# Linear attention of a two-block network: both directions' scores added before they meet the values, two heads' states on halves of the array in turn, and GpSimd as a fourth worker

## The reference, cut to what matters

```python
la_f = jax.nn.log_sigmoid((r_f @ w_decay_up[0] + b_decay[0])) / GATE_NORMALIZER      # and la_b likewise
def gla_scan(q, k, v, log_a, h0, with_output):
    b = jnp.cumsum(chunked(log_a), axis=3)
    kv = jnp.einsum('bhncd,bhnce->bhnde', kc * jnp.exp(b_last - b), vc)
    decay = jnp.exp(b_last[:, :, :, 0, :])
    # scan over chunks: state = dec_n * state + kv_n; `starts` are the states ahead of each chunk
    inter = jnp.einsum('bhncd,bhnde->bhnce', qc * jnp.exp(b), starts)
    scores = jnp.einsum('bhnid,bhnjd->bhnij', qc * jnp.exp(b - mid), kc * jnp.exp(mid - b))
    intra = jnp.einsum('bhnij,bhnje->bhnie', jnp.where(lower, scores, 0.0), vc)
    return inter + intra, final
o = o_f + rev(o_b)
o = rms_norm_2(o, gla_norm_g)        # then o * silu(g), projections, a pooling branch, merge gates, w_out
```

## Time and profile before

| | us |
|---|---|
| three runs | 4045.81, 4053.06, 4835.9; median 4053.06 |
| the profiled execution | 4056.88, its span 4055.1 |
| linear attention stage and head sums, span's 3081.40 to 3242.13 | 160.7 |
| of these, TensorE in the two head blocks | 24.4 and 25.9 |

### The profile page before, as it was taken

How to read it: one execution, slowest core, us unless ns; L and a number is a source line. 1 busy time by engine, 2 the same in 40 slices (tenths; PEclk the granted TensorE clock), 3 DMA queues, 4 the chain that set the end, 5 groups by cost and what they waited for, 6 DMA issues and landing times.

```text
span 4055.1 us, 70686 instructions
## 1 busy us (share of the span) xinstructions
PE 3674.8 (91%) x31176; PEld 2713.0 (67%) x31176; DVE 1650.1 (41%) x3233; ACT 1207.1 (30%) x2395; POOL 335.1 (8%) x512
## 2 busy tenths in 40 slices
PE   6999998999997997999999997999988898898886
PEld 2565567788885696888888886578877676532222
DVE  1253345433334443556665564344344274311112
ACT  2242033312223232444544443233343232100001
POOL 0000122000001002212121121000010001000000
PEclk9999999999998998999999999799999699889998
DMA  5293053211112010000000000222221022599996
GB/s 183 86 345 133 21 187 104 83 63 63 63 63 80 24 40 8 4 4 4 4 4 4 3 4 35 98 98 89 83 65 58 21 96 97 203 353 387 386 387 245
DMA packets 209521, 433.83 MB, mean 107 GB/s; under 512 B 4976, under 2 KB 5584, under 8 KB 208832
## 3 DMA queue, kind: packets, MB, share of 16 engines
q1 hardware_dynamic: 203952, 413.44, 28.3%
q0 software_dynamic: 5264, 15.87, 1.3%
HBM read 424.05 MB, written 5.24 MB: 106 GB/s over the span
## 4 chain that ended last, share of the span: by engine, by line
PE 75%; DVE 9%; DMA 7%; ACT 4%; SPq 3%; issue 1%; POOL 1%; DVEq 0%; ACTq 0%; POOLq 0%
PE ps L760 14%; PE ps L1918 7%; PE ps L1919 7%; PE ps L1920 7%; PE ps L2336 6%; PE ps L707 4%; PE ps L3642 3%; PE ps L690 3%; DMA part<-in_wg 3%; SPq L193 3%; PE ps L2326 2%; DMA part<-in_wd 2%; PE ps L996 1%; DMA part<-in_wu 1%; PE ps L2454 1%
## 5 line engine op out<-in xcount | busy, mean ns | idle before, releaser
L760 PE MATMUL ps<-part 128*128 128x512 f32 (+1 forms) x3312 | 631.5, 354 | 28.1 <-DVE part L981 10.9
L760 PEld LDWEIGHTS ps<-part 128*128 128x128 f32 x3312 | 538.9, 195 | 122.6 <-DVE part L981 12.1
L1918 PE MATMUL ps<-part 128*128 128x512 f32 (+1 forms) x1536 | 549.9, 358 | 18.0 <-DVE part L1965 11.4
L1919 PE MATMUL ps<-part 128*128 128x512 f32 (+1 forms) x1536 | 549.2, 358 | 0.0
L1920 PE MATMUL ps<-part 128*128 128x512 f32 (+1 forms) x1536 | 549.0, 357 | 0.0
L3642 PE MATMUL ps<-part 128*64 128x512 f32 x1536 | 383.2, 618 | 71.5 <-DMA part<-in_wd 29.9
L2336 PE MATMUL ps<-part 64*64 64x64 f32 x10752 | 365.9, 220 | 20.0 <-DVE part L2615 11.6
L2336 PEld LDWEIGHTS ps<-part 64*64 64x64 f32 x10752 | 334.5, 135 | 49.7 <-DVE part L2615 16.6
L1942 DVE TENSOR_TENSOR part<-part 128x1024 fp32r<-128x1024 f32 x128 | 158.4, 1237 | 496.6 <-ACT part L1931 496.6
L1918 PEld LDWEIGHTS ps<-part 128*128 128x128 f32 x1536 | 290.3, 189 | 68.0 <-DVE part L1965 12.6
L3642 PEld LDWEIGHTS ps<-part 128*64 128x64 f32 x1536 | 115.5, 141 | 320.3 <-issue 214.9
(11 more groups left out here) (423 smaller groups left out, 5050.7 us busy)
## 6 DMA issues: line engine op xcount, KB each, us to landing
part<-in_ada_w SPq DMA_DIRECT2D x36, 2048.0 KB, 9.0
part<-in_mlp_w SPq DMA_DIRECT2D x32, 2048.0 KB, 8.2
part<-in_wg SPq DMA_DIRECT2D x32, 2048.0 KB, 19.9
part<-in_wu SPq DMA_DIRECT2D x32, 2048.0 KB, 19.9
part<-in_wd SPq DMA_DIRECT2D x32, 2048.0 KB, 20.0
part<-in_b_in SPq DMA_DIRECT2D x8, 2048.0 KB, 8.3
part<-in_ab_w_in SPq DMA_DIRECT2D x7, 2048.0 KB, 8.8
part<-in_rkv SPq DMA_DIRECT2D x6, 2048.0 KB, 7.9
```

Of the source, the lines that this page charges most:

```text
L760: mm = pe.e.matmul(ps[:, j * n:j * n + n], lhs, rhs, start=k == ks[0] and i == 0, stop=k == ks[-1] and i == 2)
L1918: pe.e.matmul(ps, wh[:, k, :], hi[:, k, x0:x1], start=k == 0, stop=False)
L1919: pe.e.matmul(ps, wh[:, k, :], lo[:, k, x0:x1], start=False, stop=False)
```

## The change

1. **Heads.** The scores of both directions are added by GpSimd ("g scores sum") into `g.SC[0]` and `g.SC[1]`, and TensorE makes one product of values with scores for each head and 128 tokens instead of two. The two heads of a pair are made together: their state products alternate between the upper and the lower half of the array's rows, into two banks.
2. **GpSimd** takes the products of `q1` and `qm` with the queries, the sums above, clearing of two score tiles, and the second parts 6 to 9 of the weights (`Split.pool`).
3. **Logits.** ScalarE takes the absolute value straight from PSUM with the bias added (two instructions), VectorE adds the bias and takes the minimum with zero in one, so the later subtraction is a plain one.
4. **Order on TensorE.** Two gate pieces stand in turn 0, one in each turn between scores and kv, and one ahead of each head block; the transposes follow the decay logits at once. The head sums move: those of heads 0 and 1 behind kv of turn 3, those of heads 2 and 3 behind the first piece of the merge stage.
5. **Order on ScalarE and VectorE.** The masked copy of the scores comes first in a turn on VectorE. ScalarE copies the gates at the end of a turn; it copies heads 0 and 1 out in turn 3, and squares them behind that turn's exponentials; roots are taken for two heads together. VectorE scales all four heads at the stage's end.

```diff
+    def pool(self, g):                       # class Split
+        pool.wait_ge(self.K.at(name, "rounded", g))
+        pool.e.tensor_tensor(self.rest(g), self.tile(g), self.first(g), SUB).then_inc(*pool.up((name, "split", g)))
...
+GATES_IN = (2, 1, 2, 1, 2)
...
+        if step == 0:
             next(gates)
-        if step:
+            next(gates)
+        else:
...
-            pe.wait_ge(K.at("g km", dm))
+            pe.wait_ge(K.at("g qm", dm), K.at("g km", dm))
...
-            if step < 4:
-                next(gates)
+            next(gates)
...
+            if step == 3:
+                for hd in range(2):
+                    head_sum(K, hd)
             if dm % 2:
...
+                next(gates)
+                heads_pe(K, dm, m)
...
+def heads_pe(K, dm, m):
+    pe.wait_ge(K.at("g scores sum", dm))
+    out = [K.bank("g head", 2 * m + hh) for hh in range(2)]
+    pe.wait_ge(K.at("g states", dm), K.at("g q1", dm))
+    for x in range(4):
+        c = slice(x * 128, x * 128 + 128)
+        for hh in range(2):
+            hd = 2 * m + hh
+            pe.e.matmul(out[hh][:, c], g.vR[:, x, hd * 128:hd * 128 + 128], g.SC[hh][:, x, :], start=True, stop=False,
+                        skip_group_check=True)
+        for e in range(2):
+            for n in (2 * x, 2 * x + 1):
+                o64 = slice(n * 64, n * 64 + 64)
+                for hh, o in halves():
+                    mm = pe.e.matmul(out[hh][:, o64], g.ST[e][o, n, :], g.q1[(dm - 1 + e) % 3][o, o64], start=False,
+                                     stop=e == 1, skip_group_check=True)
...
-            s.e.activation(g.e1, g.la, ACT.Abs).then_inc(*s.up())
+            for pi, (a, b) in enumerate(BOTH):
+                s.wait_ge(K.at("g decay", step, pi))
+                s.e.activation(g.e1[:, a:b], K.ps.of("g decay", step, pi)[:, 0:b - a], ACT.Abs, bias=bias).then_inc(
+                    *s.up(("g abs", step, pi), free("g decay", step, pi)))
...
+        if step == 3:
+            head(0)
...
+        if step == 3:
+            head_squares(0)
+        for _ in range(GATES_IN[step]):
             gate()
...
+        if step == 3:
+            head_rstd(0)
+    head(2)
+    head_squares(2)
+    head_rstd(2)
...
+def gla_pool(K):
+    for step in range(5):
+        if step < 4:
+            pool.wait_ge(K.at("g q1 exp", step))
+            pool.e.tensor_tensor(g.q1[step % 3], g.q1[step % 3], g.qT[:, m, :], MUL).then_inc(*pool.up(("g q1", step)))
+        if step in (2, 4):
+            for hh in range(2):
+                pool.wait_ge(K.at("g scores in", dm, hh), K.at("g scores in", dm - 1, hh))
+                pool.e.tensor_tensor(g.SC[hh], g.SC[hh], g.SC[2 + hh], ADD).then_inc(*pool.up(("g scores sum", dm)))
+        if step < 4:
+            pool.wait_ge(K.at("g qm exp", step))
+            pool.e.tensor_tensor(g.qm[step % 2], g.qm[step % 2], g.qT[:, m, :], MUL).then_inc(*pool.up(("g qm", step)))
+        if step == 2:
+            pool.wait_ge(K.at("g head", 0), K.at("g head", 1))
+            for hh in range(2):
+                pool.e.memset(g.SC[hh], 0.0).then_inc(*pool.up(("g scores empty",)))
+        if step != 1:
+            w.pool((6, None, 7, 8, 9)[step])
...
-def merge_pe(K, gates):
+def merge_pe(K):
+    first = w.columns(8, "gp", 0, x, LAT, lambda k: {})
+    next(first)
+    for hd in (2, 3):
+        head_sum(K, hd)
+    through(first)
```

More of the change, by code:

```diff
@@ L3117, in gla_pe @@
[L3117 to L3120 removed]
+                next(gates)
+                heads_pe(K, dm, m)
+def heads_pe(K, dm, m):
+    g, pe = K.g2, K.pe
+    pe.wait_ge(K.at("g scores sum", dm))
[13 more added lines that the diff above has]
+                                     stop=e == 1, skip_group_check=True)
+                    if x == 3 and e == 1 and n == 7:
+                        mm.then_inc(*pe.up(("g head", 2 * m + hh)))
@@ L3123, in gla_act, with head_sum @@
+def head_sum(K, hd):
+    pe = K.pe
+    ps = K.bank("g head sum", hd)
+    pe.wait_ge(K.at("g head sq", hd))
+    pe.e.matmul(ps, K.ones, K.g2.sq1[hd % 2], start=True, stop=True).then_inc(*pe.up(("g head sum", hd)))
 def gla_act(K):
@@ L3127, in gate, with head, head_squares, head_rstd @@
     def gate():
-        m = next(gates, None)
-        if m is not None:
-            s.wait_ge(K.at("gm", m, 0))
-            s.e.activation(g.G1[:, m, :], K.ps.of("gm", m, 0), ACT.Copy).then_inc(*s.up(("gate raw", m), free("gm", m, 0)))
-            if m % 2:
-                w.act(6 + m // 2)
+        m = next(gates)
+        s.wait_ge(K.at("gm", m, 0))
+        s.e.activation(g.G1[:, m, :], K.ps.of("gm", m, 0), ACT.Copy).then_inc(*s.up(("gate raw", m), free("gm", m, 0)))
+        if m % 2:
+            w.act(6 + m // 2)
+    def head(hd0):
+        for hd in (hd0, hd0 + 1):
+            s.wait_ge(K.at("g head", hd))
+            s.e.activation(g.og[:, hd, :], K.ps.of("g head", hd), ACT.Copy).then_inc(
+                *s.up(("g head in", hd), free("g head", hd)))
+    def head_squares(hd0):
+        for hd in (hd0, hd0 + 1):
+            s.wait_ge(K.at("g head in", hd), K.at("g head gated", hd - 2) if hd >= 2 else {})
+            s.e.activation(g.sq1[hd % 2], g.og[:, hd, :], ACT.Square).then_inc(*s.up(("g head sq", hd)))
+    def head_rstd(hd0):
+        s.ln_exp()
+        for hd in (hd0, hd0 + 1):
+            s.wait_ge(K.at("g head sum", hd))
+            s.e.activation(g.sq1[hd % 2], K.ps.of("g head sum", hd), ACT.Ln, scale=1.0 / 128, bias=K.eps[:, 0:1]).then_inc(
+                *s.up(free("g head sum", hd)))
+        s.wait_ge(s.now())
+        for hd in (hd0, hd0 + 1):
+            s.e.activation(g.sq1[hd % 2], g.sq1[hd % 2], ACT.Exp, scale=-0.5).then_inc(*s.up(("g head rstd", hd)))
     for step in range(5):
@@ L3138, in gla_act @@
             d, m = DM[step]
[L3139 removed]
+            bias = g.n2[:, 29 + 2 * d + m:30 + 2 * d + m]
             if step:
@@ L3275, in merge_pool @@
     K.load(K.pool, K.po.pw, K.D["pool_w"].rearrange("g c d -> c g d"), "merge", "pw")
-def merge_pe(K, gates):
+def merge_pe(K):
     g, p, pe, w, x = K.g2, K.po, K.pe, b2(K), b2_h(K)
-    through(gates)
-    for t in range(2):
-        through(w.columns(8 + t, "gp", 2 * t, x, LAT, lambda k: {}))
+    first = w.columns(8, "gp", 0, x, LAT, lambda k: {})
[3 more added lines that the diff above has]
+    through(first)
+    through(w.columns(9, "gp", 2, x, LAT, lambda k: {}))
     for t in range(2):
```

89 lines of the change are left out of this document (24 added, 65 removed).

## The result

| | before | after |
|---|---|---|
| median, us | 4053.82 (four runs) | 4000.59 (3993.59 to 4008.23, four runs) |
| ratio | | 0.9868, 95% interval 0.9839 to 0.9897 |
| profiled execution, its span | 4056.88, 4055.1 | 3993.59, 3991.8 |
| first decay logit to first product with pool_w | 252.04 | 198.32 |

The changed kernel is 53 us faster, 1.3%, clear of no change, but less than the 2% from which a kernel is called faster here; 4003 was forecast. (One of the four runs of the kernel before, 4835.9, is disturbed and is left out of the ratio.)

What follows compares the result with a forecast made beforehand. TensorE, busy 91% of the span, was taken as the bound, through half-clock head blocks and each turn's engine ring. The stage's 277.5 to 227.1 saves 50.4 us: 4056.9 becomes 4006.5, less 3.8 gives 4003; range 3986 to 4028.

Steps and rivals of the forecast that it cites:

- TensorE's wait for VectorE in the merge: Merge stage: VectorE ends part 10 of the weights at 215.9, TensorE wants it at 215.5, so it waits 0.4 us.
- Head blocks: Two heads made together, four groups of 1.8 us: a block takes 7.1 us at full clock, the largest term.
- an estimate beside the sum: Head block by the skill's twofold gain for 64-row products: 0.13 a product, 6.7 us a block, 4002 in all.
- with neither 20: Head block with neither overlap of the array's halves nor full clock: 20 us.
- dearer heads: Rival: head blocks run at half clock or without overlap of halves, giving 4011 to 4016; chance 0.15.
- Turn 4's new wait: Behind the third kv, head sums wait for ScalarE's squares until 160.7; 12 us of the gain of 39 go back.
- clock stays up: Rival: TensorE stays at 2.4 GHz all through, taking off 9.4 us, so 3994; chance 0.14.
- Worth nothing: Ahead of the scores: moving the product of `qm` to GpSimd gains nothing, 0.6 + 1.22 replaced by 1.3 + 0.6.
- The 0.6 for `q1`: `kw` to the end of `km` on VectorE: the product of `q1` leaves it, 4.9 becomes 4.2 us.
- The lock between the two engines: GpSimd and two-SBUF-input VectorE instructions exclude each other; without it scores come 0.6 us earlier a turn, 2.4 in all.
- The second part: Weights' second parts on GpSimd take 4.6 us each; only the first delays a VectorE subtraction, by 1 us.
- the slower case: Rival: GpSimd's rounded-type write makes second parts slow; 17 us each decides it, 20 us gives 4065; chance 0.03.

Runs made afterwards that it cites:

- the heads alone: Kernel before with only the two heads of a pair made together, state products alternating halves, two products of values kept: stretch 245.60 against 252.04.
- `kw` of 3.26: Changed kernel with GpSimd's first second part of the weights moved to where VectorE makes `kw`: stretch 198.74 against 195.66.
- the slower state products: Changed kernel with state products of one head after the other, no longer alternating halves product by product: stretch 203.16 against 195.66.

## Why the prediction was right

The runs split the 56.4 us from 252.04 to 195.66, each kernel holding the last one's edits; the rows are single executions:

| step | stretch | gain |
|---|---|---|
| a gate piece ahead of heads 0 and 1 | 252.04 to 238.28 | 13.8 |
| the same for heads 2 and 3, and two heads together | to 218.62 | 19.7 |
| order of logits, sums, copies; GpSimd's other work | to 197.77 | 20.8 |
| one product of values for both directions | to 195.66 | 2.1 |

The third step is read off the kv products of the last two kernels: 3.9 us ahead of the first kv (26.1 to 22.1, 2.98 of it the wait for a bank and 0.80 one for the scores' input), 4.0 in turn 2, 14.3 to the third kv, where the sums of heads 0 and 1 and their waits no longer stand; 7.8 are given back to the fourth kv, where they stand now; 6.4 lie behind it, 1.3 in kv itself at full clock and 5.1 from the sums of heads 2 and 3 going behind the first gp piece. What within the third step belongs to which part of the change is read from places and not from runs, except for GpSimd's work above. The split holds for this order of edits; the heads alone gave 6.4 of it at the old clock.

**By the prediction's own steps**, in us from the first logit; the last two columns are the two executions of the changed kernel:

| | forecast | first | again |
|---|---|---|---|
| first kv | 22.2 | 23.7 | 22.1 |
| second kv | 42.1 | 43.7 | 41.5 |
| heads 0 and 1 | 49.9 to 57.0 | 51.2 to 57.9 | 49.0 to 55.7 |
| third kv | 69.5 | 70.4 | 68.2 |
| fourth kv | 94.4 | 91.7 | 89.0 |
| heads 2 and 3 end | 109.3 | 105.8 | 103.2 |
| TensorE's wait for VectorE in the merge | 0.4 | 0.55 | 0.55 |

The path through VectorE ahead of that last wait was right as well: from the heads' end to the last scaling 10.4 forecast and 10.4 measured, from there to the end of part 10 14.7 and 14.4.

**Head blocks.** The form of the sum was right and its result a little high: 6.69 measured, 7.1 forecast. Two products of values with the changes around them take 0.64, exactly the 2 x 0.32 of the sum. A state product is 0.13 and not the 0.14 taken from the scores, which is all of the difference; 0.13 and 6.7 a block also stood in the prediction, as an estimate beside the sum. The row of the scores, on which this term rested, was the right one. (Of the dearer cases in the prediction, "with neither 20" is wrong as a sum: half clock without overlap is 4 x (1.28 + 8 x 0.52) = 21.8. Nothing else uses it.) The rival "dearer heads" is excluded at this place (clock 1.00), but its reason is real: with the piece behind the block it comes out at 12.2.

**Turn 4's new wait.** Place, cause and length were right: still from the third kv until the squares, forecast 7.7 us (153.0 to 160.7), measured 7.60. The step that failed is the one behind it: I let sums, transposes, scores and the gate piece all run at half clock, 4.2 + 1.5 + 2.1 + 7.4, 15.2 in all. They took 3.78, 1.41, 1.16 and 5.89, 11.8 from start to start of kv: the sums started at half clock and the scores behind them ran at full. That is 3.4 of the 3.7 by which the way from the third to the fourth kv, 24.9 forecast, was shorter (21.2; in the second execution 20.8). The rival "clock stays up" was too strong (7.80 and 7.42 in turns 2 and 3), the forecast too weak.

**GpSimd.** "Worth nothing" for `qm` is borne out. The 0.6 for `q1` came as a number (`kw` to the end of `km` 4.32, forecast 4.2, before 4.87), but not for the reason given: with both products on VectorE and a wait for the first exponential alone it is 4.35. Its 0.6 shows only in turn 4's wait for the squares. The lock between the two engines, which rested on one row of another stage, was shown directly with `kw` of 3.26; the Trainium skill's SBUF — State Buffer, section "SBUF: two separate sides", says the same of two SBUF inputs, and the trace agrees. The second part was 4.52 to 4.63 us, 4.6 forecast from 256 and 512 columns; no cost of the rounded output type is seen in it, so the slower case fell. The first of them did delay one subtraction (1.52 for 0.96), with no later kv.

**The whole.** 50.4 us was forecast for the stage, 53.7 and 56.4 were measured: the mechanism held, and the sum was 3.3 to 6.0 too low, for the most part by the clock of turn 4. The medians differ by 53.2, and 4000.59 lies nearer to 4003 than the stage's terms do; that is in part luck. In the two profiled executions the total differs by 63.3; the 9.6 beyond the stretch lie almost all ahead of the stage (8.1), and are spread between executions.

## What to carry to other kernels

Independent wide products are worth more ahead of a block of small dependent ones than behind it: here the order of one piece of 5.8 us and one block decided over 26 us for two blocks, since the piece both covered the wait and let the block run at 2.4 instead of 1.2 GHz. When costing a reordering, look up the granted clock of every stretch behind the move, too. Put fillers where the trace shows a wait that a chain on other engines sets, and count also what the filler cost at the place from which it is taken (5 us in turn 3). How far behind such a piece the clock stays up is not known ahead: in the slower state products it fell within the second block. Work moved to GpSimd beside VectorE products with two SBUF inputs gained little (0.6 and 0.7 us of 56): in the chain to the scores 0.03, where waiting for the right one of two exponentials gave 0.5.

## What was not expected of the hardware

- TensorE did 24 us of small products without a gap at clock 0.50, and 12 us of them in the kernel with the piece behind; but behind the head sums (3.78) and transposes (1.41) the scores ran at full speed, and behind gate pieces every block did so at its start, to its end in all but the one of 10.4 us. What the chip goes by was not tried.
- A VectorE copy with one input, 128x12, was held as well: 1.26 us where GpSimd's product of `q1` ran (it ended 0.03 ahead of the copy's end), 0.16 to 0.17 elsewhere. The masked copy and the instruction for bias and minimum (L3257), both of which read PSUM, were not held during a second part on GpSimd: 1.41 and 1.34 for two, in the kernel before 1.38 and 1.34. Why the small copy is held is open.
- State products on the two halves of the array run fully side by side: passes start every 0.112 us on each half, and those of the other half 0.007 behind. Changes between these and the large products cost about 0.1 each, so four products on one half and eight on both take the same 1.03 with their changes.
